# Experts' input rows chosen straight into feature-major order, in a fused streaming-encoder kernel on one core

## The chip, the core and the metric

The kernel runs on one core of one Trainium2 chip. The time is the device time of one execution in microseconds (us). The kernel before takes 634.83 us, the median of 3 runs (634.35 to 634.88).

## The reference, cut to what matters

One layer of a streaming encoder is computed for 256 prompt tokens and 64 sample tokens (320 in all, width 1024): a projection, three branches (state space, latent attention, memory attention), a gated merge, and a mixture of experts. All of it is float32. Only the last part bears on this change:

```python
x = x + merged @ p["w_out"]
x = x + hierarchical_moe(rmsnorm(x, p["g_ffn"]), p)

def hierarchical_moe(h, p):
    lg = h @ p["w_rg"] + p["b_rg"]                 # 4 groups, the best one is taken
    ...                                            # top 2 of the 8 experts in that group
    gate = ...                                     # (tokens, 32), two entries per token are not 0
    for e in range(32):
        hid = silu(h @ p["w_e1"][e]) * (h @ p["w_e3"][e])      # 1024 -> 256
        y = y + gate[..., e:e + 1] * (hid @ p["w_e2"][e])      # 256 -> 1024
    return y
```

Every expert has 3 MB of weights (two matrices of 1024 x 256 for the way up, one of 256 x 1024 down), 96 MB together. They are read from HBM once, whatever the routing is.

## The kernel before, in words

The program is written engine by engine, each with its own instruction list, and semaphores between them. Nothing is scheduled by a tool: the order on an engine is the order of the code.

**Experts.** Each expert gets a block of 32 rows (B), so each token's two choices become two places `32 * expert + rank`. Four experts (128 rows) are a team, two experts a pair: there are 8 teams and 16 pairs, numbered p. A token whose rank in its expert is 32 or more goes to an overflow loop at the end, entered only where the count of overflow teams, `teams`, is over 0.

**What a team needs.** DVE builds a one-hot matrix `S` (tokens x 128 rows, three tiles of tokens: 128, 128 and 64) and a gated one, `Sg`. PE multiplies `S` by the normed tokens `h2` to get the team's 128 rows, row-major in PSUM, in two banks (`choose`, L1141, with `tile_rows`, L1124: 6 products of 512 columns per team). ACT copies them to `xg` in SBUF (`row_copies`, L1574). PE turns them to feature-major, 128 features at a time, in 8 transposes (`row_transposes`, L1180). ACT copies that to `xT` (`x_copy`, L1581). The first team has its own form: its products are spread over the routing stage tile by tile (`choose_first`, L1134), as the choice for each tile of tokens becomes known.

**What a pair does.** PE: `up` (64 products with 32 columns of `xT` as the stationary side and 256 of the weights moving), then a transpose of `hid`, then `down` (16 products of 512 columns). Between them ACT computes a tanh, DVE the two products of the SwiGLU (`hidden`), and DVE copies `hidT`. Every second pair PE also adds a team's rows back into the tokens' sums, which stay in PSUM (`add_team`), and turns `Sg` (`spread`).

**Weights.** SP issues every load. There are 7 slots of SBUF for the up weights of an expert (2 MB each) and 7 for the down weights (1 MB each). A slot is loaded again when PE has signalled the end of the product that read it: `ab_full` for up, `y_mm` for down. Experts 4 to 6's up weights wait until PE has read the last chunk of `w_out`; the down weights of expert 6 lie where `X` was and wait for `seeded`, which PE signals when it has copied all tokens into PSUM (`seed`, L1114). The first pair runs its gate half first (`first_up`, L1216), and signals it by itself as `first_gates`, so that SP can load the gate weights of experts 7 and 8 before the other half (L736 to L739).

**Order in the routing stage.** PE's list is TAIL: the products by `w_out` by tile, with transposes, router products, rank products and `choose_first` between them, then two seeds, the last tile's choice, and the last two seeds. DVE does the routing as a chain of small operations. Behind it, before the first pair, it computes where overflow rows go (L2067 to L2083); the list of overflow experts follows inside pair 0 (`overflow_teams`).

Of the kernel before, what the change touches and what calls it, by code (L numbers as in the profile page):

```python
# [17 lines left out]
ALU = mybir.AluOpType  # L18
# [382 lines left out]
def build(nc, a, o, scratch):  # L401

    ctx = ExitStack()
    with ctx:
# [6 lines left out]
        def place(at, *tensors):  # L411

            out = []
            for name, shape, *dt in tensors:
# [28 lines left out]
        (Ek, ncmp, jcmp, cnt, tp), _ = place(  # L443
            at5, ("Ek", [128, 3, NT, NE]), ("ncmp", [128, NE, NJ]), ("jcmp", [128, 2, NT, NJ]), ("cnt", [128, 4, NE]),
            ("tp", [128, 2, NT, NE]))
        (yT,), _ = place(at5 + size([128, 2, D // 2]), ("yT", [128, KD, 128]))
        (yb, xg, S, Sg, xT), at_routes = place(at5, ("yb", [128, 2, D // 2]), ("xg", [128, D]), ("S", [128, NT, 128]), ("Sg", [128, NT, 128]),
                                               ("xT", [128, KD, 128]))
# [65 lines left out]
        def const(name, rows_=128):  # L514
# [17 lines left out]
            router_ready logits_in logits_exp onehot_ready rank_full chosen ov_ready gated rows_full rows_ready weights_full weights_ready xt_full xt_ready  # L532
            ab_full tanh_ready hid_ready ht_full ht_ready y_mm y_dve y_act sum_full seeded rows_out_dve rows_out_act
            ov_w ov_chosen ov_gated ov_rows_full ov_rows_ready ov_weights_full ov_weights_ready ov_xt_full ov_xt_ready ov_ab ov_tanh ov_hid ov_ht_full ov_ht_ready ov_y_mm ov_y_dve ov_sum_full
# [250 lines left out]
        def _(pe):  # L785
# [342 lines left out]
            def rows_done(banks, full):  # L1128
                for c in range(2):
                    for t in range(NT):  # L1130
                        ins = tile_rows(banks, t, c)
                    ins.then_inc(full, 1)

            def choose_first(t, c):  # L1134
                pe.wait_ge(s["chosen"], t + 1)
                pe.wait_ge(s["h2_ready"], t + 1 + (c if t == NT - 1 else 0))
                ins = tile_rows(ROWS, t, c)
# [41 lines left out]

            def row_transposes(h, bank_, full):  # L1180

                for k in range(4):
                    ins = nc.tensor.transpose(PS[:, bank_, 128 * k:128 * k + 128], xg[:, 4 * h + k::KD], ident)  # L1183
                ins.then_inc(full, 1)

            def x_transposes(g, h):

                if h == 0:
                    pe.wait_ge(s["rows_ready"], 2 * g + 2)
                elif g > 0:  # L1190
                    pe.wait_ge(s["xt_ready"], 2 * g + 1)
                row_transposes(h, ROWS if g > 0 else ROWS + h, s["xt_full"])
# [89 lines left out]
            x_transposes(0, 0)  # L1282
            x_transposes(0, 1)
            for p in range(PAIRS):
# [22 lines left out]
                if p % 2 == 1 and p < PAIRS - 1:  # L1307
                    x_transposes(p // 2 + 1, 1)
            add_team(TEAMS - 1, range(len(SUMS)))

            with pe.If(teams > 0):
                with pe.Fori(0, OV_TEAMS) as i:
                    pe.wait_ge(s["ov_chosen"], NT * i + NT)
                    pe.sem_inc(s["pe_passed"], 1)
                    rows_done(ROWS, s["ov_rows_full"])
                    pe.wait_ge(s["ov_rows_ready"], 2 * i + 2)
                    for h in range(2):
                        row_transposes(h, ROWS + h, s["ov_xt_full"])
# [23 lines left out]
        def _(act):  # L1342
# [231 lines left out]
            def row_copies(g):  # L1574
                for h in range(2):
                    act.wait_ge(s["rows_full"], 2 * g + h + 1)
                    if g > 0 and h == 0:
                        act.wait_ge(s["xt_full"], 2 * g)
                    fn(xg[:, 512 * h:512 * h + 512], PS[:, ROWS + h, :], ACT.Copy).then_inc(s["rows_ready"], 1)

# [36 lines left out]
            row_copies(0)  # L1617
            for h in range(2):
                x_copy(0, h)
            for p in range(PAIRS):  # L1620
# [3 lines left out]
                elif p < PAIRS - 1:  # L1624
                    row_copies(p // 2 + 1)
# [8 lines left out]
            with act.If(teams > 0):  # L1634
                with act.Fori(0, OV_TEAMS) as i:
                    act.wait_ge(s["ov_rows_full"], 2 * i + 2)
                    for h in range(2):
                        fn(xg[:, 512 * h:512 * h + 512], PS[:, ROWS + h, :], ACT.Copy).then_inc(s["ov_rows_ready"], 1)
# [13 lines left out]
        def _(dve):  # L1652
# [274 lines left out]
            def normed(t, cols=slice(0, D)):  # L1927
                n = TILES[t][1]
                scaled_rows(h2[0:n, t, cols], X[0:n, t, cols], norm(("f", t)), grow[0:n, cols], s["h2_ready"])
# [137 lines left out]
            st.mark(V_.tensor_tensor(ncmp[:], n_[:, :, None].broadcast_to([128, NE, NJ]),  # L2067
# [263 lines left out]
```

## Time and profile before

| | |
|---|---|
| median of 3 runs | 634.83 us (634.35 to 634.88) |
| the profiled execution | 635.66 us, its span 633.8 us |
| PE busy, PE weight load busy | 609.9 us, 378.8 us |
| DVE, ACT, POOL busy | 291.0, 186.5, 149.2 us |
| bytes read from HBM | 147.12 MB, of which some 100 MB are expert weights |
| mean granted TensorE clock | 0.994 |

The span runs from the first to the last instruction; some 1.9 us of the execution lie around it. PE's busy time counts a matmul from its issue to a modelled end, so PE can be called busy when it does less than it could. The program has two halves: up to some 380 us the branches are computed, and from there on the merge's last product, the routing and the experts. The experts run from 426 us to 629 us of the span.

### The profile page before, as it was taken

To read this page: it belongs to the slowest core of one execution; us is meant where nothing else is said; L and a number is where in the kernel's file an instruction comes from. 1 tells how busy PE (TensorE), PEld (TensorE's weight loads), DVE (VectorE), ACT (ScalarE), POOL (GpSimd) and SP (SyncE) were. 2 spreads that over 40 slices of the span, in tenths; PEclk is the share of its full clock that TensorE was granted. 3 is DMA by queue.
4 is the path that set the end of the run, shared out by engine and by line. 5 is a ranking of instruction groups with operands and counts; after the bars stand their busy time and mean duration, and the time that the engine had idled before them with its cause. 6 is when DMAs were issued, how large, how long until landed. Compare 5 with 4: busy or idle time off the path is not lost.

```text
span 633.8 us, 9981 instructions
## 1 busy us (share of the span) xinstructions
PE 609.9 (96%) x3746; PEld 378.8 (60%) x3746; DVE 291.0 (46%) x813; ACT 186.5 (29%) x582; POOL 149.2 (24%) x341
## 2 busy tenths in 40 slices
PE   8999999999999999999999999999999999978895
PEld 7888867677456667666677767854443444434341
DVE  3343947757883589772043321675133133131302
ACT  5524224532478444423100101121221121112201
POOL 1596727733584525410000000000000000000000
PEclk9999999999899999999999999999999999989999
DMA  9793543222300343322479991099999999999993
GB/s 293 188 292 116 193 166 100 68 67 85 113 2 33 115 152 100 100 67 100 152 224 403 401 394 48 9 400 384 420 420 420 420 419 418 420 421 421 420 412 124
DMA packets 57715, 150.57 MB, mean 238 GB/s; under 512 B 12352, under 2 KB 40448, under 8 KB 45760
## 3 DMA queue, kind: packets, MB, share of 16 engines
q1 hardware_dynamic: 57664, 149.89, 63.2%
q8 instruction: 32, 0.52, 0.3%
q14 instruction: 19, 0.16, 0.1%
HBM read 147.12 MB, written 2.76 MB: 236 GB/s over the span
## 4 chain that ended last, share of the span: by engine, by line
PE 92%; DVE 3%; issue 2%; ACT 2%; DMA 1%; SPq 0%; POOL 0%; DVEq 0%
PE PS L835 28%; PE PS L845 21%; PE PS L1232 10%; PE PS L1126 7%; PE PS L1271 6%; PE PS L1261 5%; PE PS L961 2%; PE PS L918 2%; PE PS L1183 2%; PE PS L986 2%; PE PS L828 1%; PE PS L1028 1%; PE PS L969 1%; PE PS L907 1%; DMA X<-in_x_prompt 1%
## 5 line engine op out<-in xcount | busy, mean ns | idle before, releaser
L835 PE MATMUL PS<-hT,W 128*128 128x320 f32 x416 | 117.2, 436 | 0.0
L835 PEld LDWEIGHTS PS<-hT,W 128*128 128x128 f32 x416 | 77.6, 190 | 33.4 <-issue 3.8
L1232 PE MATMUL PS<-E,xT 128*32 128x256 f32 (+1 forms) x1088 | 62.8, 382 | 8.2 <-issue 7.9
L1232 PEld LDWEIGHTS PS<-E,xT 128*32 128x32 f32 x1088 | 35.9, 110 | 34.8 <-issue 15.4
L2209 POOL TENSOR_SCALAR means<-sums 128x4 f32<-128x4 f32 (+3 forms) x35 | 7.7, 221 | 187.9 <-ACT junk L1371 186.9
L1126 PE MATMUL PS<-h,S 128*128 128x512 f32 (+1 forms) x96 | 48.2, 625 | 0.3 <-DVE S L1999 0.3
L845 PE MATMUL PS<-W,hT 128*128 128x256 f32 (+5 forms) x256 | 41.7, 353 | 0.0
L1271 PE MATMUL PS<-yb,WG 128*128 128x512 f32 (+1 forms) x96 | 38.5, 609 | 0.8 <-DVE yb L2124 0.8
L845 PEld LDWEIGHTS PS<-W,hT 128*128 128x128 f32 (+1 forms) x256 | 31.5, 163 | 8.4 <-issue 1.3
L845 PE MATMUL PS<-W,mergedT 128*128 128x384 f32 (+3 forms) x192 | 35.7, 381 | 0.0
L835 PE MATMUL PS<-uT,W 128*128 128x320 f32 x128 | 34.6, 432 | 0.0
L2124 DVE COPY yb<-PS 64x512 f32<-64x512 f32 x16 | 10.9, 683 | 47.5 <-PE PS L1261 47.5
L1126 PEld LDWEIGHTS PS<-h,S 128*128 128x128 f32 (+1 forms) x96 | 15.5, 187 | 28.0 <-issue 26.8
L2210 POOL TENSOR_TENSOR rstd<-means,halves 128x4 f32<-128x4 f32 (+3 forms) x35 | 30.8, 879 | 2.9
L1261 PE MATMUL PS<-E,hidT 128*32 128x512 f32 x256 | 30.8, 598 | 0.6 <-issue 0.5
L835 PEld LDWEIGHTS PS<-uT,W 128*128 128x128 f32 x128 | 24.3, 190 | 10.1
L845 PEld LDWEIGHTS PS<-W,mergedT 128*128 128x128 f32 (+1 forms) x192 | 24.2, 163 | 9.8 <-issue 0.3
L845 PE MATMUL PS<-W,memT 128*128 128x256 f32 x128 | 28.3, 381 | 0.0
L2118 DVE COPY hidT<-PS 128x128 f32<-128x128 f32 x16 | 4.7, 292 | 50.4 <-PE PS L1241 50.4
L845 PEld LDWEIGHTS PS<-W,memT 128*128 128x128 f32 x128 | 24.1, 190 | 4.0 <-issue 0.9
L1271 PEld LDWEIGHTS PS<-yb,WG 128*128 128x128 f32 (+1 forms) x96 | 12.6, 171 | 21.4 <-issue 21.4
L2109 DVE SCALAR_TENSOR_TENSOR hid<-hid,PS 128x128 f32<-128x128 f32 x16 | 4.6, 286 | 44.6 <-ACT hid L1598 44.6
(316 smaller groups left out, 984.5 us busy)
## 6 DMA issues: line engine op xcount, KB each, us to landing
E<-in_w_e SPq DMA_DIRECT2D x93, 1024.0 KB, 23.0
W<-in_w_in SPq DMA_DIRECT2D x7, 1536.0 KB, 7.1
W<-in_w_in SPq DMA_DIRECT2D x7, 1024.0 KB, 8.1
W<-in_w_mem_kv SPq DMA_DIRECT2D x4, 1024.0 KB, 6.9
W<-in_w_glu SPq DMA_DIRECT2D x4, 768.0 KB, 8.2
W<-in_w_out SPq DMA_DIRECT2D x2, 1536.0 KB, 15.7
X<-in_x_prompt SPq DMA_DIRECT2D x4, 512.0 KB, 4.6
W<-in_w_o_mem SPq DMA_DIRECT2D x1, 1536.0 KB, 6.9
```

Source lines behind the costliest of these rows:

```text
L835: ins = mm(out[:, 0:TOK], w[:, k, cols:cols + 128], rhs[:, k, :], start=(k == 0), stop=(k == kt - 1))
L845: ins = mm(out[r:r + n, 0:part.stop - part.start], lhs[:, k, f:f + n], w[:, k, c0 + part.start:c0 + part.stop], start=(k == 0), stop=(k == ...
L918: mm(PS[:, BU, 0:TOK], wB[r:r + 32, 0, t, :], uT[r:r + 32, t, :], start=True, stop=True)
L961: ins = mm(out[n * c:n * c + n, nk * x:nk * x + nk], lhs, rhs, start=True, stop=True)
L986: ins = mm(out[w * r:w * r + w, n * i:n * i + n], values, PT[0:rows_, m % 2, at:at + n], start=(b == 0), stop=(b == len(kb) - 1))
L1126: return mm(PS[:, banks + c, :], S[0:n, t, :], h2[0:n, t, 512 * c:512 * c + 512], start=(t == 0), stop=(t == NT - 1))
L1183: ins = nc.tensor.transpose(PS[:, bank_, 128 * k:128 * k + 128], xg[:, 4 * h + k::KD], ident)
L1232: ins = mm(PS[r:r + B, AB, 128 * which.start:128 * which.stop], xT[:, k, place_ + B * n:place_ + B * n + B], E13[slot][:, which, k, j::2], ...
L1261: ins = mm(PS[r:r + B, Y, :], hidT[:, par, 64 * n + B * j:64 * n + B * j + B], E2[slot][:, j, 512 * c:512 * c + 512], start=(j == 0), stop ...
L1271: ins = mm(PS[r:r + rows_, SUM[SUMS[n]], :], WG[:, f:f + rows_], yb[:, c, :], start=first, stop=last)
L2124: V_.tensor_copy(yb[64 * (p % 2):64 * (p % 2) + 64, 0, :], PS[0:64, Y, :]).then_inc(s["y_dve"], 1)
L2210: g_.tensor_tensor(rstd[0:rows_, n, 0:heads], means[0:rows_, n, 0:heads], halves[0:rows_, 0:heads], ALU.pow)\
```

## The change

Instead of choosing rows (`S` stationary, 512 columns of `h2` moving) and turning them, the changed kernel takes 128 columns of `h2` as the stationary side (every eighth feature, `k::8`) and `S` as the moving side, 128 columns. The product is 128 features x 128 rows: already feature-major. A team takes 24 products of 128 columns (8 feature blocks k by 3 tiles of tokens) in place of 6 of 512. `row_copies`, `row_transposes` and `xg` are gone. The eight blocks are computed in two halves of four, each a whole PSUM bank. Only the first team uses two banks; later teams use one bank twice, so they no longer take the bank of Y, and the second half waits for ACT's copy of the first.

Within an odd pair, the first half's blocks 0 and 1 stand before the transposition of `hid`, blocks 2 and 3 behind it, and the second half behind `down`. DVE's last norm (64 tokens) is written in two parts by feature block instead of by column half. The overflow places move from before pair 0 to the end of pair 1 and the overflow list from pair 0 to the end of pair 3; ACT's wait for that list in pair 0 is gone. In SBUF, `yb` moves off the bytes that hold the rank counts, which now live longer.

```diff
-            def tile_rows(banks, t, c):
-                n = TILES[t][1]
-                return mm(PS[:, banks + c, :], S[0:n, t, :], h2[0:n, t, 512 * c:512 * c + 512], start=(t == 0), stop=(t == NT - 1))
...
+            def x_products(bank_, h, ks, ts):
+                for k in ks:
+                    for t in ts:
+                        n = TILES[t][1]
+                        ins = mm(PS[:, bank_, 128 * (k % 4):128 * (k % 4) + 128], h2[0:n, t, k::KD], S[0:n, t, :],
+                                 start=((k, t) == (4 * h, 0)), stop=((k, t) == (4 * h + 3, NT - 1)))
+                return ins
...
+            def choose_first(t, h):
                 pe.wait_ge(s["chosen"], t + 1)
+                pe.wait_ge(s["h2_ready"], t + 1 + (h if t == NT - 1 else 0))
+                ins = x_products(ROWS + h, h, x_half(h), (t,))
                 if t == NT - 1:
-                    ins.then_inc(s["rows_full"], 1)
-
-            def choose(g):
-                pe.wait_ge(s["chosen"], g + NT)
-                pe.wait_ge(s["weights_ready"], g)
-                pe.wait_ge(s["y_dve"], 2 * g - 1)
-                pe.wait_ge(s["y_act"], 2 * g - 1)
-                rows_done(ROWS, s["rows_full"])
+                    ins.then_inc(s["xt_full"], 1)
+
+            def choose(g, h, ks):
+                if ks[0] == 0:
+                    pe.wait_ge(s["chosen"], g + NT)
+                    pe.wait_ge(s["weights_ready"], g)
+                elif ks[0] == 4:
+                    pe.wait_ge(s["xt_ready"], 2 * g + 1)
+                ins = x_products(ROWS, h, ks, range(NT))
+                if ks[-1] % 4 == 3:
+                    ins.then_inc(s["xt_full"], 1)
...
-            x_transposes(0, 0)
-            x_transposes(0, 1)
             for p in range(PAIRS):
...
                 elif p % 2 == 1 and p < PAIRS - 1:
-                    choose(p // 2 + 1)
+                    choose(p // 2 + 1, 0, (0, 1))
                 hid_transpose(p)
...
                 elif p % 2 == 1 and p < PAIRS - 1:
-                    x_transposes(p // 2 + 1, 0)
+                    choose(p // 2 + 1, 0, (2, 3))
...
                 down(p)
                 if p % 2 == 1 and p < PAIRS - 1:
-                    x_transposes(p // 2 + 1, 1)
+                    choose(p // 2 + 1, 1, x_half(1))
...
                 act.wait_ge(s["y_mm"], p + 1)
-                if p == 0:
-                    act.wait_ge(s["ov_ready"], 2)
...
-            row_copies(0)
...
-                    row_copies(p // 2 + 1)
...
-            normed(2, slice(0, 512))
+            normed(2, slice(0, 4))
             homes(only[2], PS[:, LAST_RANKS, 0:NE])
-            normed(2, slice(512, D))
+            normed(2, slice(4, KD))
...
                 hid_copy(p)
-                if p == 0:
+                y_copy(p)
+                if p == 1:
+                    overflow_places()
+                elif p == 3:
                     overflow_teams()
-                y_copy(p)
```

**Where the instructions move.** PE in the routing stage before, from the choice for the first tile of tokens up to the first pair (`Ek` are the one-hots of the ranks, `cst` holds the identity; the moving side is named first). Lines of the order, before:

```order
L1126 MATMUL PS<-h_73,S 128x512
L1078 MATMUL PS<-cst,X 128x64 x8
...
L1126 MATMUL PS<-h_73,S 128x512 x2
L1120 MATMUL PS<-X,cst 64x512 x2
...
L1120 MATMUL PS<-X,cst 128x512 x2
L1126 MATMUL PS<-h_73,S 128x512 x2
L1120 MATMUL PS<-X,cst 128x512 x2
L1183 MATMUL PS<-cst,xg 128x128 x8
L1232 MATMUL PS<-E_0_149,xT 32x128 x2
```

The same place on PE in the changed kernel:

```order
L1130 MATMUL PS<-S,h_73 128x128 x4
L1079 MATMUL PS<-cst,X 128x64 x8
...
L1130 MATMUL PS<-S,h_73 128x128 x8
L1121 MATMUL PS<-X,cst 64x512 x2
...
L1121 MATMUL PS<-X,cst 128x512 x2
L1130 MATMUL PS<-S,h_73 128x128 x8
L1121 MATMUL PS<-X,cst 128x512 x2
L1224 MATMUL PS<-E_0_148,xT 32x128 x2
```

Every product of 512 columns has become four of 128 in the same place, and the eight transposes between the last seed and the first pair are gone.

PE in an odd pair before, between the up products of this pair and of the next:

```order
L1126 MATMUL PS<-h_73,S 128x512 x6
L1241 MATMUL PS<-cst,hid 128x128
L1183 MATMUL PS<-cst,xg 128x128 x4
L1261 MATMUL PS<-E_0_151,hidT 32x512
...
L1183 MATMUL PS<-cst,xg 128x128 x4
L1232 MATMUL PS<-E_2_153,xT 32x256 x2
```

The same place in the changed kernel:

```order
L1130 MATMUL PS<-S,h_73 128x128 x6
L1233 MATMUL PS<-cst,hid 128x128
L1130 MATMUL PS<-S,h_73 128x128 x6
L1253 MATMUL PS<-E_0_150,hidT 32x512
...
L1130 MATMUL PS<-S,h_73 128x128 x12
L1224 MATMUL PS<-E_2_152,xT 32x256 x2
```

A quarter of the choice now stands before the transposition of `hid` where all of it stood, a quarter behind it, and half behind `down`.

## Rows read from the trace of the kernel before

**Rows 1.** The page, its second part: DMA share in tenths and GB/s in 40 slices.
```profile
DMA  9793543222300343322479991099999999999993
GB/s 293 188 292 116 193 166 100 68 67 85 113 2 33 115 152 100 100 67 100 152 224 403 401 394 48 9 400 384 420 420 420 420 419 418 420 421 421 420 412 124
```
**Rows 2.** PE's waits, 430 to 634 us: total us, times, longest.
```profile
PE PS L1232 <- issue: 7.9, 5, 3.5
```
**Rows 3.** The chain that ended last: start us, us, what.
```profile
555.65 3.51 issue
559.16 5.05 PE PS L1232 x63
...
600.86 1.26 issue
...
614.92 0.92 issue
```
**Rows 4.** Windows: PE, PEld, DVE, ACT, POOL busy, then PEclk, DMA share, GB/s.
```profile
429.50:432.00 2.50, 1.39 (x36) 0.95 (x26) 0.68 (x3) 0.28 (x1) 0.00 (x0) 1.00 0.75 259
555.00:617.00 62.00, 53.27 (x427) 23.30 (x423) 14.01 (x43) 9.73 (x19) 0.00 (x0) 0.97 1.01 419
```
**Rows 5.** Timeline of SP, the issues of loads: start us, us, what.
```profile
410.39 3.11 SPq L693 DMA_DIRECT2D E<-in_w_e  x6
425.33 0.33 SPq L697 DMA_DIRECT2D E<-in_w_e  x1
428.64 3.21 SPq L739 DMA_DIRECT2D E<-in_w_e  x4
```
**Rows 6.** The chain that ended last, before the first pair.
```profile
421.40 1.98 PE PS L1126 x4
423.38 1.92 PE PS L1120 x4
425.30 0.46 PE PS L1183 x4
425.78 0.61 ACT xT L1585
...
426.52 3.95 PE PS L1232 x124
```
**Rows 7.** The chain, one odd pair from its choice on.
```profile
462.21 5.95 PE PS L1126 x12
...
486.46 5.95 PE PS L1126 x12
492.43 0.61 ACT xg L1579
493.08 0.71 PE PS L1183 x4
493.80 1.85 PE PS L1261 x16
495.65 0.64 PE PS L1183 x4
```
**Rows 8.** PE, timeline: products of 128 columns in the projection.
```profile
10.59 2.02 PE L828 MATMUL PS<-hT,W 128*128 128x128 f32 x16
```
**Rows 9.** One line's weight loads (L828): duration ns min/median/max.
```profile
L828 PEld LDWEIGHTS PS<-hT,W x64: 186/190/192, 10.6 to 20.9; 128*128 128x128 f32 x64
```
**Rows 10.** PE's groups, shapes kept apart: busy us, mean ns.
```profile
L1126 PE MATMUL PS<-h,S 128*128 128x512 f32 x64 | 32.0, 619 | 0.0
L1241 PE MATMUL PS<-cst,hid 128*128 128x128 f32 x16 | 4.9, 304 | 2.2 <-DVE hid L2111 2.2
```
**Rows 11.** A window of 1 us behind PE's longest wait, columns as in rows 4.
```profile
559.00:560.00 1.00, 0.84 (x9) 0.45 (x13) 0.97 (x3) 0.00 (x0) 0.00 (x0) 0.50 1.00 418
```
**Rows 12.** DVE's timeline: first and last of 15 overflow rows before pair 0.
```profile
425.19 0.45 DVE L2067 TENSOR_TENSOR ncmp<-cnt,cst 128x288 f32<-128x288 f32 x1
...
428.88 0.17 DVE L2083 SCALAR_TENSOR_TENSOR rs<-rs 128x6 f32<-128x6 f32 x1
```

More of the change, by code:

```diff
@@ L442, in build @@
         (gateA,), _ = place(at5, ("gateA", [128, KD, TOK]))
[L443 removed]
+        (Ek, ncmp, jcmp, cnt, tp), ranks_end = place(
             at5, ("Ek", [128, 3, NT, NE]), ("ncmp", [128, NE, NJ]), ("jcmp", [128, 2, NT, NJ]), ("cnt", [128, 4, NE]),
             ("tp", [128, 2, NT, NE]))
[L446 to L448 removed]
+        (yT,), _ = place(at5 + size([128, KD, 128]), ("yT", [128, KD, 128]))
+        assert ranks_end <= at5 + size(yT.shape)
+        (yb, S, Sg, xT), at_routes = place(at5 + size(yT.shape), ("yb", [128, 2, D // 2]), ("S", [128, NT, 128]), ("Sg", [128, NT, 128]),
+                                           ("xT", [128, KD, 128]))
         (wr, brow, lg, r8, i8, ex4, prod, gf), at7 = place(
@@ L1178, in _ @@
             pe.wait_ge(s["emptied_act"], sum(1 for _, w in UNITS if w == "act"))
[L1180 to L1192, printed above, removed]
             def weight_transposes(full):
@@ L1572, in _ @@
             xT_flat = xT[:].rearrange("p k n -> p (k n)")
[L1574 to L1579, printed above, removed]
             def x_copy(g, h):
@@ L1925, in residual, with normed @@
                             s["emptied_dve"] if part.stop == 128 * nd else None)
-            def normed(t, cols=slice(0, D)):
+            def normed(t, ks=slice(0, KD)):
                 n = TILES[t][1]
-                scaled_rows(h2[0:n, t, cols], X[0:n, t, cols], norm(("f", t)), grow[0:n, cols], s["h2_ready"])
+                dst, src, gain = (x.rearrange("p (q k) -> p q k", k=KD)[:, :, ks] for x in (h2[0:n, t, :], X[0:n, t, :], grow[0:n, :]))
+                scaled_rows(dst, src, norm(("f", t)), gain, s["h2_ready"])
             def logits(t):
@@ L2072, in _ @@
-            link(V_.tensor_tensor_scan(incl, const("ones")[:, 0:NE], nb, 0.0, ALU.mult, ALU.add))
-            link(V_.tensor_tensor(excl, incl, nb, ALU.subtract))
-            link(of_expert(ex2, excl[:, None, None, :], slice(0, NT)))
-            link(V_.scalar_tensor_tensor(ex2, ex2, float(NE - 1), j2, ALU.add, ALU.add))
-            link(V_.tensor_tensor(ex2, ex2, ek2, ALU.subtract))
-            link(V_.tensor_scalar(pos2, j2, 0.5, None, ALU.is_gt))
-            link(V_.tensor_tensor(ex2, pos2, ex2, ALU.mult))
@@ L2081, in _, with overflow_places @@
-            link(V_.tensor_tensor(ex2, ex2, ek2, ALU.add))
-            link(V_.tensor_tensor(ex2, ex2, j2, ALU.subtract))
-            link(V_.scalar_tensor_tensor(rid, ex2, float(B), rank2, ALU.mult, ALU.add))
+            def overflow_places():
+                st.mark(V_.tensor_tensor(ncmp[:], n_[:, :, None].broadcast_to([128, NE, NJ]),
+                                         const("blocks")[:, None, :].broadcast_to([128, NE, NJ]), ALU.is_gt))
+                link(V_.tensor_tensor(jcmp[:], wide(rank2, NJ), const("blocks")[:, None, None, :].broadcast_to([128, 2, NT, NJ]), ALU.is_ge))
+                st.mark(V_.tensor_reduce(nb, ncmp[:], AX.X, ALU.add))
+                link(V_.tensor_reduce(j2, jcmp[:], AX.X, ALU.add))
+                link(V_.tensor_tensor_scan(incl, const("ones")[:, 0:NE], nb, 0.0, ALU.mult, ALU.add))
+                link(V_.tensor_tensor(excl, incl, nb, ALU.subtract))
+                link(of_expert(ex2, excl[:, None, None, :], slice(0, NT)))
+                link(V_.scalar_tensor_tensor(ex2, ex2, float(NE - 1), j2, ALU.add, ALU.add))
+                link(V_.tensor_tensor(ex2, ex2, ek2, ALU.subtract))
+                link(V_.tensor_scalar(pos2, j2, 0.5, None, ALU.is_gt))
+                link(V_.tensor_tensor(ex2, pos2, ex2, ALU.mult))
+                link(V_.tensor_tensor(ex2, ex2, ek2, ALU.add))
+                link(V_.tensor_tensor(ex2, ex2, j2, ALU.subtract))
+                link(V_.scalar_tensor_tensor(rid, ex2, float(B), rank2, ALU.mult, ALU.add))
```

28 lines of the change are left out of this document (6 added, 22 removed).

## The prediction, made before the changed kernel had run

> **What bounds the kernel now.** I read the slices first. From slice 27 to 38 the DMA share is 9 in every slice and the rate stands at about 420 GB/s, while the slices before 26 swing between 9 and 400 [rows 1]. So the experts' stage is a stream of weights that moves at one rate whatever the engines do. Next came PE's waits: 7.9 us before up products, 5 times, put down to "issue", which here means a load that the profile names no releaser for [rows 2]. The chain says when: the first is at 555.65, and up to the last pair PE then waits before every up [rows 3]. A team of four experts brings 12 x 1.049 MB = 12.6 MB, at the 419 GB/s of the window [rows 4] 30.0 us. PE takes 486.46 - 462.21 = 24.25 us for a team [rows 7]. PE starts with a stock of loaded experts behind it and works in the loads' shadow, gaining 5.7 us per team until it has eaten the stock. From there on the loads lead. The end of the kernel is thus when the stream starts, plus its bytes, plus a tail after the last load. Work taken from PE, ACT or DVE inside the stage buys nothing by itself; only what makes the stream start or resume earlier does.
>
> Where does the stream have a hole? SP's issues tell it: six loads at 410.39, one at 425.33, four more at 428.64 and behind it, as PE gives the first pair's slots free [rows 5]. The six hold 6.3 MB, 15 us of stream, so they are through at some 427. Then one single load is left until those of 428.64 take effect. From 429.5 to 432 the rate is 259 GB/s where 419 is the steady one [rows 4]. That hole is the place where this change can earn, and its length hangs on when PE ends the first pair's gate half.
>
> **The change part by part.** *First team, the path to the first pair.* Before: the last tile's choice 1.98, two seeds 1.92, then 0.46 of transposes on the chain, ACT's copy 0.61, and the first up at 426.52 [rows 6]. The transposes and both row copies go. The copies to xT can now start when the last tile's first half is done, about 422.4, and finish during the seeds. So behind the seeds nothing is left: first up at 425.30, 1.22 us earlier, if 8 products of 128 columns cost what 2 of 512 did.
>
> *The new product.* The trace has its like: in the first projection, 8 products with a full 128 x 128 stationary side and 128 columns moving (16 instructions, two per float32 product) take 2.02 us, 0.253 us each [rows 8]. A product of 512 columns takes 32.0 / 32 = 1.00 us [rows 10]. Four small ones are 1.01, so the same columns cost 1% more: 24 x 0.253 = 6.06 us for 6.0 a team. Bounds: below, the same 1.00 per four (the columns streamed are equal, so no gain is to be had). Above, each product needs two weight loads of 0.19 us [rows 9]; if they ran one behind the other they would set 0.38 us per product. I take 0.253, the row with that very shape; the stride of eight floats in the stationary side is also that of the old transposes, which ran 4 in 0.64 to 0.71 us [rows 7]. On the path to the first pair 16 of the 24 count (8 before the last router products, 8 at the end), so I give back 16 x 0.003 + a little for the first loads of xT, some 0.1 us: first up at 425.4, 1.1 us earlier.
>
> The Trainium skill, "TensorE: Matmul & The Clock Gate", part 3 "The mechanism", speaks against the change: a weight load runs beside a matmul in flight only if the two use different row groups. Here all 128 rows are used, so by it load and matmul would add up, 2 x 0.19 + 0.25 = 0.63 us. The projection's row contradicts it: 16 loads of 0.19 are 3.0 us alone, and the 8 products with them took 2.02 [rows 8, 9]. It stays a rival with a small chance.
>
> *The stream.* The loads of the first pair's slots are issued 1.1 us earlier. The single load before them does not move (`seeded` comes behind the same PE work). Upper bound: all that follows is 1.1 us earlier. Lower bound: in the time won, DMA was not idle but at 259 of 419 GB/s, so only 1.1 x (1 - 259/419) = 0.42 us of stream is new. Between them I take 0.8, as the resumed loads fill engines that had run dry and what is left of the single load fits into their ramp.
>
> *Later teams.* On the chain, ACT's 0.61 and the transposes' 0.71 and 0.64 go, 1.96 us [rows 7]; choice +0.06; and `hid`'s transposition, 0.30 [rows 10], hidden behind ACT's copy before, now stands in the chain. Saved: 1.6 us per team, 7 times. All of it turns into waiting for loads. PE's waits before up should rise from 7.9 to about 7.9 + 7 x 1.6 + (1.1 - 0.8) = 19 us, less what a low clock eats, and the first should come well before 555. At pair 11, which it reached at 555.65, PE would arrive 1.1 + 5 x 1.6 = 9.1 earlier, at 546.5, with the load there at 559.16 - 0.8 = 558.4: 11.9 us of lead. PE now gains 30.0 - 22.65 = 7.3 us per team, so the lead begins 1.6 teams or 49 us earlier, around 510 (between 505 and 530).
>
> *Waits added.* The second half of a choice waits for the copy of the first. That copy (0.6 us) falls under `down` (1.85 us), so it is free. Choice no longer waits for Y's copies. Only a quarter of the choice now covers tanh and products of `hid` (6 x 0.253 = 1.5 us); where nothing covers them, in two of the 16 pairs, PE stood 2.2 us in all, 1.1 each [rows 10], so the cover holds; without it the cost is under 1 us of PE time that the loads hide anyway.
>
> *DVE.* The 15 overflow rows, 425.19 to 429.05 [rows 12], ended before the first pair's `hid` at 430.5 (426.52 + 3.95 [rows 6]), and would with first up 1.1 us earlier still end 0.3 us before it: worth nothing, in or out. In pair 1 they stand behind `y_copy`: 0.7 us of copy (the page) and 3.9 of places make 4.6, while PE has half a choice (3.0) and an up (about 3.9) to do before pair 2's `hid` is wanted. The list in pair 3 is shorter and has the same room. `ov_ready` is read by PE at the last pair, by far later. The norm in two strided parts has the same elements; I count 0.
>
> *Sum.* -0.8 us. The profiled execution: 635.66 - 0.8 = 634.9, span 633.0. Its own time stands 0.8 above the median of the runs, so the median comes to 634.83 - 0.8 = 634.0 us.
>
> **The rivals.**
> *A. Nothing is gained in the stream.* The hole would be the single load's own slowness and not a lack of issued loads. For it: DMA share is 0.75 in the hole, so the engines are not empty [rows 4]. Against: 25% are. Time: 634.8.
> *B. More is gained.* All 1.1 us of shift, and the saved PE time frees slots earlier so that small dips behind 432 close too. For it: the rate in slice 27 is 384 [rows 1]. Against: from slice 28 the stream has no dip. Time: 634.83 - 1.1 - 0.3 = 633.4.
> *C. Weight loads bind the small products (the slower side).* Place: the 16 products on the path to the first pair. Price at 0.38 us each: 16 x 0.13 = 2.0 us later, less 1.1 = 0.9 at the first pair, and the single load, which hangs on the same PE work, 2.0 later with an idle stream before it: about +1.3 in the stream. Each team then costs 24 x 0.13 - 1.6 = 1.5 us more on PE, 10 over seven teams, which eats the 7.9 us of waits and adds some 0.5. Time: 636.5. It decides from 0.25 + 1.1/16 = 0.32 us per product on. At 0.63 us (the rule that the skill states) PE would carry 24 x 0.38 - 1.6 = 7.5 us more a team, 52 in all, minus 8, plus 5 at the front: some 680 us. The shape's own row is against both.
> *D. The clock.* PE's longest wait, 3.5 us, was followed by a granted clock of 0.50, that is 1.2 GHz [rows 11], and the up behind it took 5.05 us where the first pair's, with the same columns in all, took 3.95, +1.1 [rows 3, 6]. With 19 us of waits there will be several such. All but the last are hidden, for they only shorten the next wait. One before pair 14 is not: PE waited 1.26 there [rows 3], 2.8 with the change, and the next wait is only 0.92, so 1.1 - 0.9, or 0.3 us with rounding up, reach the end: 634.3. A wait before the last pair stays at 0.9, since pair 14 has no choice to save.
>
> **How the numbers follow.** Forecast 0.50 (its own range 633.3 to 634.6, with 0.3 for the scatter of medians), D 0.10, A 0.17, B 0.12, C 0.08 (636.5) and 0.01 at the skill's price; 0.02 for what I don't see. About 0.2% (1.27 us, below 633.56) is what a measurement can tell from no change. The upper bound of the shift is just under it, so only B and the lower edge of the forecast pass: 0.12 + 0.18 = 0.30 faster. C and half of what I don't see are slower, 0.12 with a little for a tail that I misread. The rest, 0.58, is no change. The range 633.0 to 635.8 holds the forecast, D, A and B; it leaves out C and some of B.
>
> **What would show it.** Right: first up near 425.4; choice products at 0.25 us each; four load issues at about 427.5; the rate from 429.5 to 432 well over 259; the rate 420 unbroken to the end; PE's waits before up near 19 us; ACT and PE less busy by 16 copies' and 64 transposes' time without a trace in the end. Wrong: choice products over 0.32 us; the hole as long as before although issues came earlier (A); a granted clock under 1 in the last pair; the first wait still near 555.

## The result, and the profile after

| kernel | median us (range) | profiled span | granted clock |
|---|---|---|---|
| before | 634.86 (634.35 to 636.44) | 633.8 | 0.994 |
| after | 702.33 (702.15 to 703.46) | 700.5 | 0.925 |

The change makes the kernel slower: 1.1062 times the time, 95% interval 1.1039 to 1.1084, or 67.5 us by the medians. (The median of before is that of four runs here, of three where it stands above.) The forecast was 634.0 us, its range ended at 635.8, and slower had a chance of 0.12. It was wrong in sign and in size.

The page, its second part, of after (TensorE's busy share, the granted clock in tenths, GB/s):

```profile
PE   8999999999999999999999999999999999999995
PEclk9999999999999999999999988878888888978789
GB/s 297 153 265 137 242 119 67 62 77 102 10 21 240 92 83 69 90 137 250 400 400 281 1 237 218 424 348 421 309 424 315 419 318 419 266 422 272 112 1 78
```

Where before's rate stood at 420 without a break from slice 28 on [rows 1], it now swings between 266 and 424: the stream of weights pauses because no slot is free. No wait before an up-projection is left on TensorE, where before had 7.9 us [rows 2]. These are all its waits from 430 us on (total us, times, longest):

```profile
PE PS L1233 <- DVE hid L2088: 2.1, 2, 1.0
PE PS L1263 <- DVE yb L2101: 0.8, 1, 0.8
PE PS L1253 <- issue: 0.5, 1, 0.5
```

So the bound has moved from the memory to TensorE. The chain of waits, one team late in the stage (start us, us, line and count; L1130 is the choice, L1233 the transposition of `hid`, L1253 down, L1224 up; sums and the weights' transposes stand in the gap):

```profile
615.47 3.63 PE PS L1130 x12
619.10 0.26 PE PS L1233
619.36 3.83 PE PS L1130 x12
623.19 3.34 PE PS L1253 x16
626.53 7.77 PE PS L1130 x24
634.30 4.80 PE PS L1224 x61
...
644.28 1.85 PE PS L1253 x16
646.13 3.62 PE PS L1224 x64
```

The next choice starts at 646.13 + 3.62 = 649.75. From one to the next this is 34.3 us (33.9 to 35.0 between the other choices), where it was 24.25 [rows 7]. The choice takes 3.63 + 3.83 + 7.77 = 15.23 us for 24 products, 0.63 us each; before it took 5.95. That is 9.28 of the 10.04 us. The rest: copy and transposes -1.96, `hid`'s transposition +0.26, and, without one product more, the down behind the choice +1.49 (3.34 against 1.85) and the up behind it +1.0. At the front the path to the first pair reads:

```profile
416.99 4.14 PE PS L1130 x16
...
424.74 4.10 PE PS L1130 x16
428.84 3.31 PE PS L1121 x4
432.15 0.36 PE PS L1224 x7
```

The last tile's choice takes 4.10 us, where two 512-column products took 1.98, and the seeds 3.31 in place of 1.92 [rows 6]. First up is at 432.15, not 426.52. Together: 5.6 at the front, 7 x 10.04 = 70.3 in the teams, less the 7.9 us of waits that are gone [rows 2], less 1.2 for the up that a low clock had stretched in before [rows 3]: 66.8 us. The spans differ by 66.7.

What is different inside the choice is seen in the weight loads (duration ns min/median/max), where before's L1126 had a median near 0.19 us, as L828 [rows 9]:

```profile
L1130 PEld LDWEIGHTS PS<-S,h x384: 308/334/353, 408.9 to 667.9; 128*128 128x128 f32 x128, 64*128 64x128 f32 x64
```

### The profile page after: what moved, and what is told of

Read it like the earlier page. It is cut to its first block, busy times and chain, and to the rows that moved or that the text cites. A ratio compares the mean times of both kernels' runs of the same rounds, so it can differ in the third digit from the quotient of the medians.

```text
span 700.5 us, 10398 instructions
## 1 busy us (share of the span) xinstructions
PE 687.4 (98%) x3970; PEld 456.5 (65%) x3970; DVE 291.1 (42%) x813; ACT 177.3 (25%) x566; POOL 148.6 (21%) x341
## 4 chain that ended last, share of the span: by engine, by line
PE 95%; DVE 2%; DMA 2%; ACT 1%; issue 0%; SPq 0%; DVEq 0%
PE PS L836 25%; PE PS L846 19%; PE PS L1130 17%; PE PS L1224 10%; PE PS L1253 6%; PE PS L1263 5%; PE PS L962 2%; PE PS L919 2%; PE PS L987 1%; PE PS L829 1%; PE PS L1029 1%; PE PS L970 1%; PE PS L1121 1%; DMA W<-in_w_in 1%; PE PS L1090 1%; PE PS L908 1%
## 5 line engine op out<-in xcount | busy, mean ns | idle before, releaser
L1130 PE MATMUL PS<-S,h 128*128 128x128 f32 (+1 forms) x384 | 120.9, 458 | 0.0
L1130 PEld LDWEIGHTS PS<-S,h 128*128 128x128 f32 (+1 forms) x384 | 100.2, 328 | 29.8 <-issue 23.3
L1224 PE MATMUL PS<-E,xT 128*32 128x256 f32 (+1 forms) x1088 | 69.3, 411 | 0.0
L1224 PEld LDWEIGHTS PS<-E,xT 128*32 128x32 f32 x1088 | 36.3, 118 | 33.7 <-issue 16.7
L1253 PE MATMUL PS<-E,hidT 128*32 128x512 f32 x256 | 41.5, 780 | 0.6 <-issue 0.5
L1566 ACT ACTIVATE xT<-PS 128x512 f32<-128x512 f32 x16 | 9.6, 597 | 109.1 <-PE PS L1130 109.1
L836 PEld LDWEIGHTS PS<-uT,W 128*128 128x128 f32 x128 | 24.3, 190 | 10.1
```

Source lines behind the costliest of these rows:

```text
L836: ins = mm(out[:, 0:TOK], w[:, k, cols:cols + 128], rhs[:, k, :], start=(k == 0), stop=(k == kt - 1))
L1130: ins = mm(PS[:, bank_, 128 * (k % 4):128 * (k % 4) + 128], h2[0:n, t, k::KD], S[0:n, t, :], start=((k, t) == (4 * h, 0)), stop=((k, t) == ...
L1224: ins = mm(PS[r:r + B, AB, 128 * which.start:128 * which.stop], xT[:, k, place_ + B * n:place_ + B * n + B], E13[slot][:, which, k, j::2], ...
L1253: ins = mm(PS[r:r + B, Y, :], hidT[:, par, 64 * n + B * j:64 * n + B * j + B], E2[slot][:, j, 512 * c:512 * c + 512], start=(j == 0), stop ...
L1566: fn(xT_flat[:, 512 * h:512 * h + 512], PS[:, ROWS if g > 0 else ROWS + h, :], ACT.Copy).then_inc(s["xt_ready"], 1)
```

## The experiments

Three theories fit these rows. T1: the stride of eight floats makes each weight load slow, and the loads set the pace. T2: the shape (many products of 128 columns, each with two new loads) is what costs. T3: the granted clock, 0.81 in the stage, is the cause and not a result.

**e1_contiguous: the stride alone taken away.** The norm writes `h2` block by block, so that a block's 128 features lie side by side.

```
- dst, src, gain = (x.rearrange("p (q k) -> p q k", k=KD)[:, :, ks] ...
+ dst = h2[0:n, t, :].rearrange("p (k q) -> p k q", k=KD)[:, ks]     # src, gain: "p (q k) -> p k q"
- mm(PS[...], h2[0:n, t, k::KD], S[0:n, t, :], ...
+ mm(PS[...], h2[0:n, t, 128 * k:128 * k + 128], S[0:n, t, :], ...
```

> The changed kernel, except that the last norm writes h2 with each block of 128 features (every eighth feature) in one piece, so that the stationary side of the 24 choice products is read without a stride. Same products, same order. Theory T1 (the stride of eight floats makes the weight load 0.33 us instead of 0.19, and two loads of it set the product): loads back at 0.19, a product at 0.25 us, no low clock in the choice, first up near 425.4, time 633.5 to 635. Rival T2 (the shape sets it: 128 columns moving behind a full weight load, or the one-hot as the moving side): products stay near 0.51 to 0.60 us and the time near 700. Rival T3 (the clock fell first and the loads are slow for it): loads 0.33 again wherever the granted clock is low.

Measured: 636.46 us (634.66 to 638.9), ratio 1.0021 (1.0005 to 1.0037), clock 0.996. The loads:

```profile
L1130 PEld LDWEIGHTS PS<-S,h x384: 182/189/250, 409.2 to 603.3; 128*128 128x128 f32 x128, 64*128 64x128 f32 x64
```

Some 66 of the 67.5 us are gone with the stride, so T1 holds and T3 falls: the clock came back by itself. The 633.5 to 635 us expected were missed all the same: it is slightly slower than before (0.2%), not faster. Three rows of it say where to look: a team's choice still takes 8.26 us, not 6.1; the norm's passes on VectorE, which now read with a stride, take 2.12 us where they took 1.29; and near the end a wait of 1.79 is followed by a down of 3.29:

```profile
485.75 2.11 PE PS L1130 x12
...
488.12 1.92 PE PS L1130 x12
...
491.89 4.23 PE PS L1130 x24
```
```profile
594.39 1.79 issue
596.19 3.29 PE PS L1253 x16
```

**e2_before_split128: the shape alone, without the stride.** The kernel before, each 512-column product split into four of 128, the one-hot side loaded again for each.

```
+ for j in range(4):
+     mm(PS[:, banks + c, 128 * j:...], S[0:n, t, :], h2[0:n, t, 512 * c + 128 * j:... + 128], ...
```

> The kernel before, with every choice product of 512 columns made as four of 128 with the same stationary side S (contiguous) loaded again for each. It has the small shape and the extra loads, but no stride. T1: a product of 128 columns takes 0.25 us, four take 1.0, and the time is that of before, 634 to 636. T2: 0.51 us each, a team's choice 12 us instead of 6, PE bound, near 660 or more.

Measured: 634.84 us (633.08 to 638.11), ratio 1.0000 (0.9982 to 1.0017). Its choice, the same 24 products with 48 loads as the changed kernel:

```profile
485.94 6.15 PE PS L1127 x48
```
```profile
L1127 PEld LDWEIGHTS PS<-h,S x384: 182/192/192, 409.1 to 594.9; 128*128 128x128 f32 x128, 64*128 64x128 f32 x64
```

0.256 us each. T2 falls, and with it the view that load and product add up when they share their rows: the 48 loads of 0.19 us alone make 9.1 us, and all of it took 6.15.

**e3_strides: how the load grows with the stride.** Block k of the changed kernel is read at a stride of k + 1 floats (so other features are chosen).

> The changed kernel, but feature block k is read with a stride of k+1 floats (1 to 8) from the start of h2, each on a line of its own, so other features than the right ones are chosen; the first half's last tile waits for the whole norm. One look at the duration of the loads by stride. T1 in its bank form: 0.19 us for odd strides, longer for 2, 4 and most for 8. T1 in its row form (the load reads lines of 32 or 64 bytes and every line costs): the duration grows with the stride, 0.19 at 1 and 0.33 at 8. T2 and T3: no dependence on the stride.

Measured in a single run: 679.17 us. The loads of strides 1 to 8, in order (ns min/median/max, of which I read the medians; strides 6 and 7, left out, are at 318 and 324):

```profile
L1133 PEld LDWEIGHTS PS<-S,h x48: 183/188/337, 410.8 to 630.7; 128*128 128x128 f32 x32, 64*128 64x128 f32 x16
L1135 PEld LDWEIGHTS PS<-S,h x48: 189/196/333, 411.0 to 631.8; 128*128 128x128 f32 x32, 64*128 64x128 f32 x16
L1137 PEld LDWEIGHTS PS<-S,h x48: 248/261/331, 411.2 to 633.2; 128*128 128x128 f32 x32, 64*128 64x128 f32 x16
L1139 PEld LDWEIGHTS PS<-S,h x48: 305/328/332, 411.6 to 634.9; 128*128 128x128 f32 x32, 64*128 64x128 f32 x16
L1141 PEld LDWEIGHTS PS<-S,h x48: 291/316/321, 414.1 to 638.5; 128*128 128x128 f32 x32, 64*128 64x128 f32 x16
...
L1147 PEld LDWEIGHTS PS<-S,h x48: 309/335/341, 415.5 to 644.1; 128*128 128x128 f32 x32, 64*128 64x128 f32 x16
```

188, 196, 261, 328, then flat: the load grows until every float lies in another 16 bytes and no further. A clash of banks at powers of two would have set 2, 4 and 8 far apart from 3, 5 and 7. Strides 4 and 8 are only 11 to 12 ns above 5 and 7, and 2 is below 3.

The Trainium skill, "SBUF — State Buffer", section "Door 1: The DMA port swizzle", says that the on-chip memory has lines of 16 bytes and that at least two accesses to each line are needed for full bandwidth. Strides 1 and 2 (four and two floats to a line) at 188 and 196 ns, 3 at 261, 4 and more at 316 to 335 agree with it. Another figure in that section of the Trainium skill, that float32 can be strided by 4 for free, does not hold for these loads: 328 ns at a stride of four. The rule of two accesses to a line spoke against the change, and the prediction did not weigh it.

**e4_wide: is it the clock or the loads?** The stride stays; each product moves 256 columns, the one-hot block twice, so the array has more to do behind each load (sums land in two blocks, so the result is another).

> The changed kernel with S streamed twice per product (256 columns moving, added into the wrong blocks), stride of eight kept. The load still takes 0.33 us, the moving columns now 0.5 us per product. If the low clock of the changed kernel comes from a PE array that idles behind loads (T4), the granted clock stays at 1.00, down after the choice takes 1.85 us instead of 3.3 and up 3.8 instead of 4.8, a product stays at 0.51 to 0.60, and the time falls from 702 by about 7 x 3 to 5 us, to 670 to 685, although the kernel computes twice the columns. If the clock has another cause, the low clock stays and the time is 702 or more.

Measured: 688.31 us (687.44 to 690.32), ratio 1.0844 (1.0817 to 1.087), clock 0.996. Twice the columns, and 14 us faster than the changed kernel, if above the 670 to 685 us expected: a product of a team took 0.67 us, not 0.51 to 0.60. One team:

```profile
475.14 4.07 PE PS L1130 x12
...
479.47 3.85 PE PS L1130 x12
483.32 1.85 PE PS L1254 x16
485.17 8.13 PE PS L1130 x24
493.30 3.76 PE PS L1225 x64
```

The choice is a little longer (16.05 for 15.23), but down and up behind it are back at 1.85 and 3.76. So the low clock is a result and not the cause: in the changed kernel it came with products of 128 columns behind slow loads, and with products of 256 columns behind the same loads (median 334 ns in both) it did not come. That the array stands idle behind the loads is the theory that foretold this; no row shows the idle time, and the row of TensorE's busy share shows 9 throughout.

The same run shows that the loads set the pace. On the path to the first pair, where a choice stays within one tile, e4's 8 products of 256 columns take 4.12 us, and the changed kernel's 8 of 128 took 4.14 and 4.10:

```profile
417.70 4.12 PE PS L1130 x16
...
425.30 4.12 PE PS L1130 x16
```

Within one tile the choice of the changed kernel takes the same at either level of the clock, too. Its first 4 products (8 instructions, below) and its 8 for the second tile of tokens (4.14 us, above) have the same form. The first two windows lie in these, the third in the choice for the last tile (PE, PEld, DVE, ACT, POOL busy, then PEclk, DMA share, GB/s):

```profile
408.93 2.10 PE PS L1130 x8
```
```profile
408.90:411.00 2.10, 2.10 (x11) 1.98 (x9) 1.36 (x6) 1.15 (x2) 0.00 (x0) 1.00 0.56 82
417.00:421.00 4.00, 4.00 (x16) 3.84 (x16) 3.35 (x20) 0.31 (x2) 0.00 (x0) 0.50 1.01 426
424.80:428.80 4.00, 4.00 (x17) 3.78 (x17) 3.53 (x14) 0.60 (x1) 0.00 (x0) 0.93 0.18 76
```

That is 0.52 us per product at 1.00 and at 0.50. So the price of the clock is paid in the main by what comes next: 2.5 us per team, 7 times, and 1.4 at the seeds, some 19 us of the 67; e4 less its own 7 x 0.8 of longer choices says 14 + 5.7 = 20. A small part may lie in the choice of the later teams, where the tiles alternate. Its second quarter takes 3.83 us for 3.63 in the first, while in e4, at a clock of 1.00, it is the shorter one (3.85 for 4.07). If all of a choice kept to e4's proportions, that would be 0.9 us per team, an estimate from these rows.

**e5_tiles_outer: what was left over in e1.** Products run over all blocks of one tile before the next; the norm reads in order and writes with a stride.

```
- dst = h2[...].rearrange("p (k q) -> p k q")[:, ks]    # src, gain: "p (q k) -> p k q"
+ dst = h2[...].rearrange("p (k q) -> p q k")[:, :, ks] # src, gain: "p (q k) -> p q k"
- for k in ks:
-     for t in ts:
+ for t in ts:
+     for k in ks:
```

> The changed kernel with the features of a block laid side by side in h2 (stationary side without a stride), as in the first experiment, but with two differences from it: the norm on VectorE reads its input in order and writes with the stride (there it read with a stride of eight and wrote in order, and its 128x1024 pass rose from 1282 to 2106 ns), and the products run over all blocks of one token tile before the next tile (there tile 0 and 1 and 2 alternated within a block, and 24 products took 8.26 us, 0.344 each, against 0.256 each in the split 512-column products of the kernel before). Theory 1 (what was left of the cost in the first experiment is the changes between tiles of 128 and 64 rows): the choice falls to 6.1 to 6.6 us per team, a team lasts about 22.7 us where transfers allow, norm passes are back at about 1.28 and 0.74 us, first up-projection about 1 us earlier relative to the issue of the first expert loads, time 633.5 to 635.5, ratio 0.998 to 1.001. Rival (the cost is in the number of loads or in two halves of the choice, not in the order): choice stays at 8 to 8.3 us. Rival for the end: with a shorter choice TensorE waits longer for the last loads, the granted clock falls to 0.5 in a pause before the last down-projections, and the time stays at 636 or more.

Measured: 634.89 us (633.54 to 638.74), ratio 1.0008 (0.9991 to 1.0026).

```profile
483.27 1.73 PE PS L1130 x12
...
485.26 1.53 PE PS L1130 x12
...
488.65 3.07 PE PS L1130 x24
```

The choice takes 1.73 + 1.53 + 3.07 = 6.33 us, as the first theory had it; a team takes 22.9. The part on the norm missed: written with a stride it costs nearly as much (2.05 us) as read with one (2.12). In the changed kernel, where `h2` has the order of its source and the pass runs in order on both sides, it takes 1.29, as before. The pass of the changed kernel and that of e5:

```profile
401.07 1.29 DVE L1645 SCALAR_TENSOR_TENSOR h<-X,rstd,grow 128x1024 f32<-128x1024 f32 x1
```
```profile
402.89 2.05 DVE L1645 SCALAR_TENSOR_TENSOR h<-X,rstd,grow 128x1024 f32<-128x1024 f32 x1
```

So the stride has a price on VectorE too, 0.8 us for 128 x 1024 on either side; it is paid on two such passes and two smaller ones, not on 192 products.

**e12_alternate_full: which change between tiles costs.** As e5, but the two tiles of 128 rows alternate at every product, and the tile of 64 rows follows alone.

> The kernel of e5_tiles_outer with another order of the 24 products of a choice: the two tiles of 128 rows alternate at every product (block by block), then the tile of 64 rows is gone through alone. The first experiment had all three tiles alternating and 0.344 us per product; with the tile outermost it was 0.26. If any change of the stationary side's tile costs, a team's choice is 7 us or more here (16 of 24 products follow a change). If only the change between 128 and 64 rows costs, it stays at 6.3 to 6.5 us, since that change comes as seldom as in e5_tiles_outer. The time of the kernel, near 635 us in either, says nothing.

Measured in a single run: 635.76 us, and the choice is 1.73, 1.53 and 3.07 us, equal to e5's to the last digit. So it costs nothing to change between tiles of 128 rows. What costs is the change between 128 and 64 rows: e1 makes 7 such within its 12 last products and needs 4.23 us, e5 makes 1 and needs 3.07, so about 0.19 us each. The first quarter says the same: 3 changes and 2.11 us in e1, 1 and 1.73 in e5 (an estimate from these rows). The changed kernel has the order of e1.

**e6_overflow_early: the overflow lists back in their old place, on top of e5.**

> The kernel of e5_tiles_outer with the overflow places and the list of overflow teams computed where the kernel before has them (ahead of and behind the first pair), and ACT waiting for the list at the first pair. If moving them behind pairs 1 and 3 is worth nothing, as the prediction has it, the time agrees with e5_tiles_outer within 0.2% (1.3 us) and the first y copies of VectorE are later by a microsecond or two with no PE wait for them. If the move was worth something, this one is slower by over 0.2%, with a PE wait for y before the down-projection of pair 1.

Measured: 635.43 us (633.64 to 638.13), ratio to before 1.002 (1.0004 to 1.0037). It is 0.5 us above e5, and the two intervals overlap. Its trace has no wait of TensorE before a down that e5's lacks. The move is worth nothing that can be told.

**e8_filled: is it the low clock near the end that keeps e5 from being faster?** Four products of no use are put into the waits at pair 13.

> The kernel of e5_tiles_outer with four 128x512 products of no use (results overwritten): two ahead of the up-projection of pair 13 and two ahead of the wait for loads in the down-projection of pair 13, where the first experiment had waits of 2.34 and 1.79 us, and after the second of them a granted clock of 0.50 for 4 us (down-projection 3.29 us, not 1.85). Theory: the clock stays at 1.00 to the end, the down-projection of pair 13 takes 1.85 us and the end comes 1 to 2 us earlier than in e5_tiles_outer, if that one shows the low clock; time 632.5 to 634.5. Rival: the last loads bind in either, so the filled products change nothing (within 0.2%); or they delay work that was not waiting, and the time is up to 2 us longer.

Measured: 634.73 us (633.35 to 636.8), ratio 1.0005 (0.9989 to 1.0022). The down of pair 13 in e5, and in this kernel, with the start of the last up:

```profile
594.38 2.59 issue
596.97 3.50 PE PS L1253 x16
...
616.31 3.74 PE PS L1224 x61
```
```profile
596.62 1.92 PE PS L1259 x16
...
614.35 1.78 issue
616.13 3.93 PE PS L1224 x62
```

The clock was kept (1.92 for 3.50), and with a down that also began 0.35 us earlier, TensorE was at the last up 1.9 us sooner. All but 0.2 of that came back as a wait of 1.78 for the last loads, which e5 does not have there. The last up starts at the same time within 0.2 us. The rival held: the stream binds either way.

**e9_before_half_loads and e10_contig_half_loads: what would the change be worth if memory did not bind?** Both load only half of the bytes into the reused weight slots, but for the last expert's up weights (the sums are others).

```
- ((0, KD),)                      ->  + ((0, KD if e < UPS else KD // 2),)
- E2[e % DOWNS][:, j0:j1, :]      ->  + E2[e % DOWNS][:, j0:j1, 0:(1024 if e < DOWNS else 512)]
```

> The kernel before with half the bytes of each expert's weights that is loaded into a reused buffer (experts behind the first ones get blocks 0 to 3 of 8 of the up-projection and 512 of 1024 columns of the down-projection; the rest stays what the buffer held, so the sums are others). Instructions of TensorE are the same. With transfers out of the way the end stage is bound by TensorE: the waits before up-projections (some 12 us from 555 us on) go and the time is about 621 to 625 us. It is the base for the next kernel.

> The changed kernel with contiguous features and tiles outermost (e5_tiles_outer), with the same half of the weight bytes left out. Theory (the change without the stride does shorten TensorE's work, and the memory takes the gain in the full kernel): a team takes 22.9 us and not 24.3 by the rows of the two traces, over 7 teams 9 us less, so this one ends 6 to 10 us earlier than e9_before_half_loads, at 613 to 618 us. Rival (nothing was saved: what the row copies and transposes cost came back in the halves of the choice): within 1.3 us of e9_before_half_loads.

Measured: 625.31 us (624.59 to 626.32) and 614.01 us (613.73 to 614.87); ratios to before 0.984 (0.9808 to 0.9873) and 0.9656 (0.9626 to 0.9686). Neither chain has a wait for loads left before an up. With the transfers out of the way the contiguous form is 11.3 us faster, a little over the 6 to 10 expected: the work that the change saves on TensorE is real. A team takes 24.3 us in e9 (choices start at 485.08 and 509.41) and 22.9 in e10 (482.11 and 505.01), 7 times 1.4 = 9.8, which the spans (622.7 and 613.1) repeat. In the full kernel, where e5 stands at 1.0008 of before, the weights' stream takes all of it.

**e13_after_half_loads: have the transfers a part in the 67 us?** The same half left out of the changed kernel.

> The changed kernel itself (stride of eight kept) with the same half of the weight bytes left out as in e9_before_half_loads. If its end stage is bound by TensorE alone, as no wait ahead of an up-projection in its trace says, the time stays at 698 to 704 us while the kernel before fell by 10 us and the contiguous one by 21 us. If the transfers had a part in the 67 us (weight tiles arriving late, or reads of the on-chip memory shared with them), it falls by more than 5 us, and loads of 330 ns get shorter.

Measured: 700.65 us (700.15 to 701.15), median load 334 ns as before. It falls by 1.7 us, where e10's fell by 20.9. But for those 1.7 us the changed kernel is bound by TensorE alone.

**e11_moving_strided: the stride on the other side.** As e2, one-hot side loaded in order, the features on the moving side read with a stride of eight (rows are copied in another order of features).

```
- h2[0:n, t, 512 * c + 128 * j:512 * c + 128 * j + 128]
+ h2[0:n, t, 4 * c + j::KD]
```

> The kernel before with its 512-column products split into four of 128 (as in e2_before_split128, 634.84 us), the one-hot side stationary and contiguous, and the features on the moving side read with a stride of eight floats (rows are copied with their features in another order, so the sums are others). If a stride costs on the stationary side alone, loads stay at 190 ns, the choice at 48 instructions in about 6.15 us (0.256 each), time within 0.3% of 634.8. If any strided read by TensorE costs, the choice is 8 to 12 us and the time 650 us or more.

Measured: 691.04 us (686.95 to 692.66), ratio 1.0877 (1.0839 to 1.0916), clock 0.952.

```profile
475.03 11.98 PE PS L1127 x48
```
```profile
L1127 PE MATMUL PS<-h,S x384: 407/412/585, 408.9 to 648.4; 128*128 128x128 f32 x128, 64*128 64x128 f32 x64
```

I had expected the stride to cost on the stationary side alone. It costs on either: 11.98 / 24 = 0.50 us per product here, and 4.10 / 8 = 0.51 with the stride in the loads, against 0.256 with none. With a stride of eight floats on either operand, one pass of 128 columns (a product is two) takes 0.25 us instead of 0.128.

## Why the prediction was wrong

The step that failed is "*The new product*". It took 0.253 us from a row "with that very shape" [rows 8]. The shape was right, and e2 shows that the shape costs just that (0.256). The access was not: that row's stationary side lies in order. With the stride a product took 0.51 us within one tile and 0.63 in a team's choice, and its loads 334 ns where 190 were taken. The stride was put aside in half a sentence, since the old transposes had it too and "ran 4 in 0.64 to 0.71". But nothing was compared with them. The trace of before held a transpose of the same kind that loads in order, the weights' at L1197: its loads have a median of 140 ns, those of the strided ones at L1183 193 ns. The size could not be had from that (53 ns there, 144 in the products: 334 against 190; why the transposes pay less is open), but that the stride has a price could, and the changed kernel makes 384 such loads.

Of the other steps:

- *The sum for later teams* (choice +0.06, saved 1.6 us, PE's lead growing by it) stands or falls with the product. In e5, without the stride, a team takes 22.9 us where 22.65 was forecast: choice 6.33 for 6.06, transposition 0.26 for 0.30.
- *First team*: forecast first up 1.1 us earlier. In e5 it comes 0.6 earlier, counted from the issue of the six loads (426.30 - 410.79 = 15.5 us, before 16.1). What is missing stands in two rows: the choice for the last tile starts 0.35 us later, behind the half of the norm with the stride (1.02 us on the chain for 0.65), and takes 2.24 us for 1.98; 1.22 - 0.35 - 0.26 = 0.61. The rate from 429.5 to 432 is 357 GB/s for 259 [rows 4]. So the hole does close in part.
- *The stream*, -0.8 us in all: not confirmed. The saved work did turn into waits: in e5 12.1 us before ups and 3.1 before downs, where 19 were forecast, the first at 525.4 for 510. -0.8 us would be a ratio of 0.9987; e5 and e8 stand at 1.0008 and 1.0005, and their intervals begin at 0.9991 and 0.9989. What was won in the hole does not show in the start of the last up. Where those 0.6 us go is open; the runs of one kernel scatter by more (633.54 to 638.74 in e5).
- *Waits added* and *DVE*: right, as far as the runs tell. `hid` costs TensorE 2.1 us in all as before (2.2), and the overflow lists' place nothing (e6).
- *The norm*, counted 0: right in the changed kernel (1.29 us in both), though called strided, which its passes of 128 x 1024 are not; where one side is, it costs 0.8 us (e1, e5).
- *Rival C* had the right mechanism, loads that set the pace (e4), and the wrong price. It let them rise only to 0.38 us per product, two loads of 0.19, and gave the 0.63 that a team's product did cost a chance of 0.01. The reason it had for 0.63 was wrong: no run shows load and product adding up when the loads lie in order. The cost at 0.63 is made of 0.51 for the stride and 0.12 besides. The changes between 128 and 64 rows would make 0.10 of that, 13 in 24 products at 0.19 us, if they cost as much behind strided loads as in e1; no run shows them there. Its sum for this price comes to 634.8 + 52 - 8 + 5 = 684, not the "some 680" written. From there to 702 are 18 us, and they are the clock's (19 to 20 by the rows above).
- *Rival D* priced the low clock behind waits. It does come there (in e5 a wait of 4.05 is followed by an up of 5.44 for 3.8), and behind slow loads as well, without any wait.
- A reading of [rows 1] was loose: before slice 26 the rate swings between 2 and 403 GB/s, not 9 and 400. Nothing in the sum hangs on it.

The rival that was missing is a new access pattern on a known shape.

## What to carry to other kernels

A duration is borrowed from a row of the same shape and the same access pattern, on both operands; the step between elements in bytes belongs to the form of an instruction, though the profile's form does not print it. If TensorE must read every eighth float many times, let another engine lay the data in order once: here passes of VectorE that cost 0.8 us more per 128 x 1024 made each of 192 products 0.25 us shorter. That brought the kernel back to the time of before (e5), not below it. And before work is taken off an engine, halve the transfers in an experiment: it tells in one pair of runs (11.3 us against 0) whether the engine or the memory would take the gain.

## What the runs showed that I had not expected

- With a stride of eight float32 a product of TensorE takes twice as long, on the stationary side (0.51 us for 0.256) and on the moving side (0.50). By the loads of the stationary side the price is full as soon as each element lies in another 16 bytes (328 ns for 188), and there is hardly any at a step of 8 bytes (196). On the moving side only the stride of eight was measured.
- Within one tile such products take as long at a granted clock of 0.50 as at 1.00 (0.52 us each) and with 256 columns moving as with 128 (4.12 us and 4.14 for eight). The clock was low behind them: down 1.85 to 3.34, up 3.8 to 4.8. With twice the columns moving per load the clock stayed at 1.00 and the kernel was 14 us faster.
- Changing between tiles of 128 and of 64 rows costs about 0.19 us each time; changing between two tiles of 128 rows costs nothing.
- On VectorE a pass of 128 x 1024 took 2.12 us with a strided read (32 bytes), 2.05 with a strided write (512 bytes), and 1.29 in order.
